# Gates of 16384 experts built per token for all 128 key columns inside the hidden stage of a fused two-block transformer kernel

## The reference, cut to what matters

```python
    experts = jnp.take_along_axis(cand_i, pos, axis=-1)      # i1 * 128 + i2, 8 heads x 16
    gates = jax.nn.softmax(top_s, axis=-1)
...
        u = u_tab[ec].astype(f32)
        act = jax.nn.gelu(jnp.einsum('ced,cd->ce', u, xc.astype(f32))) * gc
        return jnp.einsum('ce,ced->cd', act, v_tab[ec].astype(f32)).astype(x.dtype)
```

## Time and profile before

| what | us |
|---|---|
| median of 3 runs | 2077.47 |
| lowest, highest | 2070.85, 2085.71 |
| profiled execution, its own time | 2075.43 |
| its span | 2073.6 |

### The profile page before, as it was taken

One profiled execution on the slowest core, in us unless ns is written; L12 is line 12 of the kernel. 1 busy time (PEld: TensorE's weight loads), 2 busy tenths in 40 slices (PEclk: granted clock), 3 DMA queues, 4 the chain that ended last, 5 costly groups with the idle time before them and its releaser, 6 DMA issues.

```text
span 2073.6 us, 29276 instructions
## 1 busy us (share of the span) xinstructions
PE 1791.5 (86%) x11704; PEld 1539.8 (74%) x11704; DVE 1485.7 (72%) x2190; ACT 844.1 (41%) x1373; POOL 1081.6 (52%) x560
## 2 busy tenths in 40 slices
PE   5998998899899976978979989888887877779997
PEld 4667997677699955656669989888787655557886
DVE  6655767555467567776552797889999999996444
ACT  4444664344366523124332544433332333334553
POOL 3212677231156813574143565578888666665443
PEclk9999999898799987888589999999999999999999
DMA  5413554452155534223134656443444333335664
GB/s 208 143 61 122 173 188 147 157 159 71 35 197 186 172 123 146 66 77 107 46 95 149 203 163 176 150 129 127 140 126 138 106 122 122 120 117 169 190 197 143
DMA packets 77319, 283.33 MB, mean 137 GB/s; under 512 B 8704, under 2 KB 8960, under 8 KB 76800
## 3 DMA queue, kind: packets, MB, share of 16 engines
q1 hardware_dynamic: 75888, 275.97, 42.0%
q10 hardware_dynamic: 1296, 5.49, 0.7%
HBM read 279.33 MB, written 2.10 MB: 136 GB/s over the span
## 4 chain that ended last, share of the span: by engine, by line
DVE 45%; PE 43%; ACT 4%; issue 4%; POOL 3%; DMA 1%; POOLq 0%; DVEq 0%; SPq 0%; ACTq 0%
PE bank L449 35%; DVE xs L1105 17%; DVE wl L1099 9%; PE bank L440 5%; DVE H L1105 3%; DVE tab L1105 2%; ACT wh L831 2%; PE bank L532 2%; DVE att L1110 1%; DVE ssb L1105 1%; DVE acl L1105 1%; DVE att L1116 1%; POOL wl L1692 1%; ACT att L834 1%; DVE ssv L1452 1%
## 5 line engine op out<-in xcount | busy, mean ns | idle before, releaser
L1692 POOL TENSOR_TENSOR wl<-raw,wh 128x1024 fp32r<-128x1024 f32 x253 | 678.9, 2690 | 538.2 <-ACT wh L831 538.2
L831 ACT ACTIVATE wh<-raw 128x1024 fp32r<-128x1024 f32 x515 | 531.1, 1048 | 174.7 <-PE bank L449 166.3
L449 PE MATMUL bank<-hh,wh 128*128 128x256 f32 x1904 | 548.3, 288 | 23.4 <-DVE hl L1105 17.3
L449 PE MATMUL bank<-hl,wh 128*128 128x256 f32 x1904 | 540.7, 284 | 0.0
L449 PE MATMUL bank<-hh,wl 128*128 128x256 f32 x1904 | 538.5, 283 | 0.0
L1099 DVE TENSOR_TENSOR wl<-raw,wh 128x1024 fp32r<-128x1024 f32 x262 | 415.6, 1595 | 146.4 <-ACT wh L831 146.3
L449 PEld LDWEIGHTS bank<-hh,wh 128*128 128x128 f32 x1904 | 366.4, 192 | 25.9 <-issue 14.3
L449 PEld LDWEIGHTS bank<-hl,wh 128*128 128x128 f32 x1904 | 366.7, 193 | 0.0
L449 PEld LDWEIGHTS bank<-hh,wl 128*128 128x128 f32 x1904 | 366.1, 192 | 0.0
L1105 DVE TENSOR_TENSOR xs<-sta,xs 128x512 bf16<-128x512 bf16 (+1 forms) x256 | 359.1, 1441 | 1.4 <-POOL xs L1697 1.4
L1697 POOL TENSOR_TENSOR xs<-xs 128x768 bf16<-128x768 bf16 x128 | 224.7, 1755 | 131.8 <-DVE xs L1105 130.8
(11 more groups left out here) (180 smaller groups left out, 2384.6 us busy)
## 6 DMA issues: line engine op xcount, KB each, us to landing
raw<-in_ut_dram SPq DMA_DIRECT2D x128, 512.0 KB, 4.0
raw<-in_vt_dram SPq DMA_DIRECT2D x128, 512.0 KB, 3.6
raw<-in_wup_dram SPq DMA_DIRECT2D x88, 512.0 KB, 4.2
raw<-in_win_dram SPq DMA_DIRECT2D x48, 512.0 KB, 4.6
raw<-in_wdown_dram SPq DMA_DIRECT2D x44, 512.0 KB, 3.6
raw<-in_wout_dram SPq DMA_DIRECT2D x24, 512.0 KB, 3.7
raw<-in_wga_dram SPq DMA_DIRECT2D x16, 512.0 KB, 3.6
raw<-in_wpq_dram SPq DMA_DIRECT2D x16, 512.0 KB, 4.0
```

What stands on the lines that cost most here:

```text
L449: m = p.e.matmul(out, lhs[i][a], rhs[i][b], start=start and i == 0 and j == 0, stop=stop and i == n - 1 and j == 2)
L831: a.e.activation(high_of(u), raw_of(u), ACTF.Copy).then_inc(act_hi.up(("hi", u)), 1)
L1692: g.e.tensor_tensor(low_of(u), raw_of(u), high_of(u).bitcast(F32), ALU.subtract).then_inc(pool_lo.up(("lo", u)), 1)
```

## The change

All gates are made inside the hidden stage, for all 128 columns i2 at once.

- Routing is due at units 29 and 58 (`J_SEL`). Lower halves of units 0 to 59 are all made by POOL, those of units 60 to 127 all by DVE.
- From unit 60 on (`J_GATE`) each unit is followed by the gates of one group of 4 tokens, 64 groups in all. The one-hots of a token are four tensor_scalar on VectorE, 128x128 bf16 each: one compares the row of numbers with the token's `sel1`, three compare it with `sel2` and multiply by one part of `selG`, scalars read from memory, one value per partition. They lie in 9 buffers. POOL has no part in it.
- PE makes the gates of a group with 12 matmuls of 128 columns into one of banks 2, 3, 6, 7; hidden units take banks 0, 1, 4, 5.
- DVE multiplies the gates of columns already activated into H (`gates_in`, 61 to 124 columns x 4 tokens). ACT copies the gates of the columns still to come into the free places of H (`Gs`, from 67 down to 4 columns x 4 tokens). When such a column's activation is made, ACT writes the gelu of the tokens that have their gates back into PSUM and of the rest into H, and DVE multiplies the former by the stored gates (`gated_hidden`).
- The output stage has no gates left.

```diff
+        J_SEL = (29, 58)
+        J_GATE, N_GR = 60, 64
+
+
         lower = []
         for i in range(n_units):
             d2 = first["wga"] - 8 <= i < first["wglu"] - 2
-            if first["ut"] <= i < first["ut"] + 66:
-                lower.append("pd"[(i - first["ut"]) % 3 == 1])
+            if first["ut"] <= i < first["ut"] + J_GATE:
+                lower.append("p")
+            elif first["ut"] <= i < first["vt"]:
+                lower.append("d")
             elif i >= first["ut"]:
                 lower.append("dp"[i % 2])
...
-        ohA = [xs[:, 640 + 256 * j:896 + 256 * j].bitcast(BF16).rearrange("p (t n) -> p t n", t=4) for j in range(2)]
-        ohB = xs[:, 1152:1280].bitcast(BF16).rearrange("p (t n) -> p t n", t=4)
-        ohG = [xs[:, 1280 + 384 * j:1664 + 384 * j].bitcast(BF16).rearrange("p (s t n) -> p s t n", s=3, t=4) for j in range(2)]
+
+        oneh = [xs[:, 640 + 256 * j:896 + 256 * j] for j in range(5)] + [oh_s[:, 256 * j:256 * j + 256] for j in range(4)]
+        oneh = [a.bitcast(BF16).rearrange("p (s n) -> p s n", s=4) for a in oneh]
+        N_OH = len(oneh)
+
+
+        def gate_bank(g):
+            return (2, 3, 6, 7)[g % 4]
+
+        def hid_bank(j):
+            return (0, 1, 4, 5)[j % 4]
+
+        def gated_before(j):
+            return min(max(j - J_GATE, 0), N_GR)
...
             def claim(b):
                 if emptied[b]:
                     p.wait_ge(emptied[b][0], *emptied[b][1:])
+                if also[b]:
+                    p.wait_ge(also[b][0], *also[b][1:])
+                    also[b] = None
...
             def hidden(j):
-                i, b = first["ut"] + j, j % 2
+                i, b = first["ut"] + j, hid_bank(j)
                 unit(i)
                 claim(b)
                 m = mm3(banks[b][:, 0:256], [unit_pair(i, k, 8, tcols(0)) for k in range(8)], [hT(k, ALLC) for k in range(8)], True, True, ready_both(("f", 2)))
                 m.then_inc(pe_out.up(("used", i), ("hid", j)), 1)
-                emptied[b] = (act_out, ("H", j))
+                emptied[b] = (dve_out, ("HG", j)) if gated_before(j) else (act_out, ("H", j))
...
-            def gates_of(i):
-                b = 2 + i % 2
+            def gates_of(g):
+                b = gate_bank(g)
                 claim(b)
-                p.wait_ge(dve_out, ("ohA", i))
-                p.wait_ge(pool_out, ("ohG", i))
-                for j in range(4):
-                    m = mm(banks[b][:, j * 64:(j + 1) * 64], [(ohA[i % 2][:, j, :], ohG[i % 2][:, s_, j, :]) for s_ in range(3)])
-                m.then_inc(pe_out.up(("G", i)), 1)
-                emptied[b] = (dve_out, ("G", i))
+                for t in range(4):
+                    k = 4 * g + t
+                    p.wait_ge(dve_out, ("oh", k))
+                    o = oneh[k % N_OH]
+                    mm(banks[b][:, t * 128:(t + 1) * 128], [(o[:, 0, :], o[:, 1 + s_, :]) for s_ in range(3)]
+                       ).then_inc(pe_out.up(("Gt", k), ("G", g) if t == 3 else None), 1)
+                emptied[b], also[b] = (dve_out, ("G", g)), (act_out, ("Gs", g))
 
             def down(js):
                 for t in range(2):
@@ -798,19 +822,13 @@
...
             for j in range(128):
-                if j == 31:
-                    sel_turned(0)
-                if j == 63:
-                    sel_turned(1)
+                if j in J_SEL:
+                    sel_turned(J_SEL.index(j))
                 hidden(j)
-                if j >= 65:
-                    gates_of(j - 65)
-            gates_of(63)
-            for j in range(128):
-                if j < 64:
-                    gates_of(64 + j)
-                if j < 126:
-                    down([j])
+                if 0 <= j - J_GATE < N_GR:
+                    gates_of(j - J_GATE)
+            for j in range(126):
+                down([j])
             down([126, 127])
...
                 stream(first["ut"] + j)
+
+                n, b = 4 * gated_before(j), hid_bank(j)
                 a.wait_ge(pe_out, ("hid", j))
                 if j * 256 + 256 > R_AT:
                     a.wait_ge(dve_out, ("selG", 1))
-                do(H[:, j, :], banks[j % 2][:, 0:256], ACTF.Gelu_apprx_tanh, ("H", j))
+                if n < 256:
+                    do(H[:, j, n:256], banks[b][:, n:256], ACTF.Gelu_apprx_tanh, ("H", j))
+                if n:
+                    do(banks[b][:, 0:n], banks[b][:, 0:n], ACTF.Gelu_apprx_tanh, ("H", j))
+                g = j - J_GATE
+                if 0 <= g < N_GR:
+                    a.wait_ge(pe_out, ("G", g))
+                    do(H[:, j + 1:128, 4 * g:4 * g + 4], banks[gate_bank(g)][:, :].rearrange("p (t j) -> p j t", t=4)[:, j + 1:128, :],
+                       ACTF.Copy, ("Gs", g))
 
             def split_gated(j):
-                a.wait_ge(dve_out, ("G", 63 + 64 * (j // 64)))
+                a.wait_ge(dve_out, ("G", N_GR - 1), ("HG", 127))
...
-            def one_hot(i):
-                half, g = i // 64, i % 64
-                ts4 = slice(4 * g, 4 * g + 4)
-                v.wait_ge(dve_out, ("selG", 1))
-                if i >= 2:
-                    v.wait_ge(pe_out, ("G", i - 2))
-                tt(ohA[i % 2], iob.unsqueeze(1).broadcast_to([128, 4, 128]), sel1[:, ts4].unsqueeze(2).broadcast_to([128, 4, 128]), ALU.is_equal,
-                   ("ohA", i), alone=True)
-                if i:
-                    v.wait_ge(pool_out, ("ohG", i - 1))
-                tt(ohB, iob[:, 64 * half:64 * half + 64].unsqueeze(1).broadcast_to([128, 4, 64]), sel2[:, ts4].unsqueeze(2).broadcast_to([128, 4, 64]),
-                   ALU.is_equal, ("ohB", i), alone=True)
-
-            def gates_of(i):
-                half, g = i // 64, i % 64
-                if i == 0:
-                    one_hot(0)
-                    one_hot(1)
-                hv = H[:, 64 * half:64 * half + 64, 4 * g:4 * g + 4]
-                v.wait_ge(pe_out, ("G", i))
-                v.wait_ge(act_out, ("H", 64 * half + 63))
-                tt(hv, hv, banks[2 + i % 2][:, 0:256].rearrange("p (t j) -> p j t", t=4), ALU.mult, ("G", i), alone=True)
-                if i < 126:
-                    one_hot(i + 2)
+            def one_hots(g):
+                for k in range(4 * g, 4 * g + 4):
+                    o = oneh[k % N_OH]
+                    v.wait_ge(dve_out, ("selG", 1))
+                    if k >= N_OH:
+                        v.wait_ge(pe_out, ("Gt", k - N_OH))
+                    v.e.tensor_scalar(o[:, 0, :], iob, sel1[:, k:k + 1], None, ALU.is_equal).then_inc(dve_out.up(), 1)
+                    for s_ in range(3):
+                        v.e.tensor_scalar(o[:, 1 + s_, :], iob, sel2[:, k:k + 1], selG[:, s_, k:k + 1], ALU.is_equal, ALU.mult
+                                          ).then_inc(dve_out.up(("oh", k)), 1)
+
+            def gates_in(g):
+                n = J_GATE + g + 1
+                hv = H[:, 0:n, 4 * g:4 * g + 4]
+                v.wait_ge(pe_out, ("G", g))
+                v.wait_ge(act_out, ("H", J_GATE + g))
+                tt(hv, hv, banks[gate_bank(g)][:, :].rearrange("p (t j) -> p j t", t=4)[:, 0:n, :], ALU.mult, ("G", g), alone=True)
+
+            def gated_hidden(j):
+                n = 4 * gated_before(j)
+                if n:
+                    v.wait_ge(act_out, ("H", j))
+                    tt(H[:, j, 0:n], H[:, j, 0:n], banks[hid_bank(j)][:, 0:n], ALU.mult, ("HG", j), alone=True)
 
             steps = routing(0)
             for j in range(128):
-                if j == 31:
+                if j in J_SEL:
                     for _ in steps:
                         pass
-                    sel_turned(0)
-                    steps = routing(1)
-                if j == 63:
-                    for _ in steps:
-                        pass
-                    sel_turned(1)
+                    sel_turned(J_SEL.index(j))
+                    steps = routing(1) if j == J_SEL[0] else iter(())
                 next(steps, None)
                 stream(first["ut"] + j)
-                if j >= 65:
-                    gates_of(j - 65)
-            gates_of(63)
+                g = j - J_GATE
+                if 0 < g <= N_GR:
+                    gates_in(g - 1)
+                gated_hidden(j - 1)
+                if 0 <= g < N_GR:
+                    one_hots(g)
+            gated_hidden(127)
...
             split_gated(0)
             for j in range(128):
-                if j < 64:
-                    gates_of(64 + j)
                 if j + 1 < 128:
                     split_gated(j + 1)
...
-            def one_hot(i):
-                g4 = i % 64
-                g.wait_ge(dve_out, ("ohB", i))
-                if i >= 2:
-                    g.wait_ge(pe_out, ("G", i - 2))
-                tt(ohG[i % 2], ohB.unsqueeze(1).broadcast_to([128, 3, 4, 64]), selG[:, :, 4 * g4:4 * g4 + 4].unsqueeze(3).broadcast_to([128, 3, 4, 64]),
...
             for j in range(128):
```

(28 more changed lines are left out.)

## The result

| | before | after |
|---|---|---|
| median of the executions (us) | 2078.6 (4 runs, 2070.85 to 2085.71) | 2159.22 (4 runs, 2152.28 to 2162.19) |
| profiled execution / its span (us) | 2075.4 / 2073.6 | 2158.43 / 2156.5 |
| mean granted clock of PE | 0.936 | 0.914 |

The change makes the kernel slower: ratio 1.0369, 95% interval 1.0332 to 1.0407. The forecast was 2108 us, slower by 1.5%: the sign was right, and the loss came out at 3.7%.

A forecast was written before the change was run, and what follows sets the result against it. VectorE was taken to bound both gate stages, PE the rest. Unit 60's activation at 1327.6, 64 rings of 6.36 (407), output from 1745, 348 for output, 12.3 tail and 1.8 over the span gave 2108 us; range 2045 to 2160.

The forecast's parts named there:

- Part 1: Output stage without gates: its first 63 units also go at 2.72 us each, gaining 103.5 us.
- Part 2: Units 0 to 59: POOL keeps up with all lower halves, and shorter waits at the expert picks gain 11.6 us.
- The stalls: Pauses between activations at the two expert picks, forecast at 5 us each, 21.6 together before.
- Part 3: Units 60 to 123: each gate group waits for the one before, 6.36 us each, 64 times.
- the ring: Circle of waits from PE through ACT and a whole DVE step back to PE, 6.36 us (5.30 to 6.92).
- The fixed part: Everything in one circle of waits in units 60 to 123 except the 16 one-hots: 3.56 us.
- the size of s: Step of one one-hot on DVE in units 60 to 123: 0.175 us in the mean, ends 0.109 and 0.21.
- The second rival's first half: One-hots' second scalar costs as much as the first: s 0.21, ring 6.92, total 2143; chance 0.20 shared with PE's clock falling.
- The clock half of that rival: PE's clock falls while it idles in units 60 to 123: total 2140; chance 0.20 shared with the second scalar's cost.
- The other rivals: Scalar reads partly or wholly hidden (0.22; wholly: 2040 us), ring open (0.05), or no change from rings of 5.6 to 6.2.
- The ring did not open: Rival for units 60 to 123: something runs a step ahead, DVE's sum of 4.58 us bounds, total 1994; chance 0.05.
- the 0.144: One-hot step in us at which the old time is met; below it scalar reads hide enough to be faster.

The follow-up runs named there:

- e4: The kernel after with every third lower half of units 0 to 59 back on DVE, the rest on POOL: 2166.97 us, ratio 1.0448 to the kernel before.
- e2: The kernel after with each group's one-hots moved to the start of DVE's step, same instructions: 2038.94 us, ratio 0.9821 to the kernel before.
- e1: The kernel after with the constant 0.0625 as second scalar in 12 of 16 one-hots: 2102.36 us, ratio 1.0106 to the kernel before.
- e3: e2 with every second lower half of units 60 to 127 made by POOL: 2073.07 us, ratio 0.9956 to the kernel before.
- e6: The kernel after, its order kept, with two f32 one-hots per token for four bf16: 2068.71 us, ratio 0.9913 to the kernel before.
- e5: e2 with two f32 one-hots per token for four bf16, one f32 matmul for three: 1945.04 us, ratio 0.9346 to the kernel before.

## Why the prediction was right or wrong

- **Part 1 held.** 128 output units in 348.1 us (348), PE the only bound, DVE under half busy.
- **Part 2 was too hopeful by 4.7 us.** The stalls are 14.7 and not 10. That POOL keeps up held: units between the picks stand 2.80 apart, and e4 puts 17 us on the assignment.
- **Part 3: the ring closes, as read from the code.** The chain, the idle time of DVE (1.73 for 1.7) and DVE's share (75% for 73%) are as forecast; e2 moves the 16 one-hots ahead and DVE's wait is gone. The fixed part comes to 6.92 - 16 x 0.208 = 3.59, forecast 3.56.
- **The step that failed is the size of s**: "Twelve of the 16 have two such scalars, which no row shows: 0 to 59 ns more ... I take 0.175 as the mean, near the row." The one-scalar step was 0.163 (0.168 worked out), but the second scalar costs 0.060, the upper end, and twelve of sixteen have it. The mean is 0.208, and the ring 6.92. The second rival's first half had s 0.21 and the same 6.92. The trace had one neighbour for the term, the 59 ns of a first scalar, and by it the mean would have been 0.212. The 0.175 left the second scalar some 9 ns, close to nothing, with no row behind it. e1 shows this cause alone, 0.72 us a period with the second scalar a constant.
- **The clock half of that rival fell.** The clock did fall (0.89), for some 3.4 us at a time in about every second period. But even behind such a dip, from 1508.7 on, PE waits for DVE ahead of the last three tokens' matmuls (0.26, 0.49 and 0.49 us), and e4 has the same period at 0.93.
- **The other rivals fell.** The ring did not open, and s stayed far above the 0.144 below which the scalars would have been hidden enough for a gain.
- **What no part foresaw**: 10.9 us ahead of the hidden stage.

The sum in the prediction's own marks, profiled execution: unit 60's activation came at 1341.6, forecast 1327.6. Of these 14.0 us, 10.9 lie ahead of the first hidden weight and 4.7 in the stalls, less some 1.6 for a quicker first unit and for units 2.80 apart and not 2.83. From it to the first output matmul 454.4 us passed, forecast 417.4: 37.0 more, 64 x 0.56 = 35.8 of it the rings. 0.53 of each 0.56 is s (16 x 0.033), 0.03 the fixed part. Output stage and tail agree within 0.4. Together 50.9 us, the distance of 2158.4 from 2107.5. With the ring at its measured 6.92 the same sum gives 2143. The other 15 us lie in the stalls and in the low clock of the attention. That clock is in the profiles of the kernel after, e1, e3 and e6 and not in those of the kernel before, e2, e4 and e5. Whether the edits have a part in which execution has it stays open. The ten executions of e3 alone go from 2052.84 us at a mean clock of 0.928 to 2079.21 at 0.914, so one kernel can differ that much from itself; where in the program they part is not on record.

## What to carry to other kernels

When no engine is full, write the order of every engine's list as a circle and ask what the last instruction of a step waits for: here a swap of a few lines on one engine was worth 115 us, and with it the change that had lost 3.7% gained 1.8%, and 6.5% with fewer one-hots. For many small instructions with one term unknown, price each operand by its nearest neighbour in the trace and multiply by the count before taking it for nearly nothing. An idle engine is free only if it shares nothing with the busy one: time the pair side by side first.

## What the runs showed that was not expected

- A tensor_scalar of 128x128 bf16 steps in 0.163 us with one scalar read from memory and in 0.223 with two. With a constant in place of the second it is 247 ns long and not 309. By the formula of the Trainium skill (VectorE: DVE Perf Modes, the section on the TRN2 errata) an estimate is 94 ns, and this trace does not agree. The same section warns that many small tiles pay a fixed cost each, and there the trace agrees: a 128x4 form takes 170 ns already.
- Output in f32 and not bf16 adds only 31 ns to it (280 and 341 against 249 and 309), though the bytes written double.
- A bf16 one-hot that meets POOL's product of 1024 elements takes 2.37 us and not 0.31.
- In four of the eight profiled executions PE's clock was low for 37.5 us on end in the attention of layer 0, where the code is alike, and the first hidden weight came 6 to 19 us later in those (1132.1, 1132.2, 1133.8 and 1140.0 against 1121.2 to 1125.9).
